# A gathered part of the expert sum grows from 512 to 768 columns and moves to SBUF, with the first norm's rows made in the query stage

## What is computed

```python
h = _layer_norm(DEEPNORM_ALPHA * h + mix, ln1_g[l], ln1_b[l])
ffn = _peer(h, w_peer_q[l], peer_subkeys[l], peer_u[l], peer_v[l])
h = _layer_norm(DEEPNORM_ALPHA * h + ffn, ln2_g[l], ln2_b[l])

# _peer: 8 heads x 16 picks a token, of 128 x 128 experts
q = (xt @ w_q).reshape(t, PEER_HEADS, 2, PEER_QDIM // 2)
scores = jnp.einsum('thpd,hpkd->thpk', q, subkeys)
...                       # top 16 of each half, top 16 of their sums
act = jax.nn.gelu(jnp.einsum('tkd,td->tk', u_tab[eb], xb))
out = jnp.einsum('tk,tkd->td', gb * act, v_tab[eb])
```

## Time and profile before

| | us |
|---|---|
| median of 3 runs (lowest, highest) | 1992.04 (1989.96, 1997.78) |
| the profiled execution | 1982.38 |
| its span, first to last instruction | 1980.5 |
| PE busy | 1945.3 (98%) |
| DVE busy | 1314.3 (66%) |
| POOL busy | 1427.6 (72%) |
| ACT busy | 989.6 (50%) |

### The profile page before, as it was taken

How to read it: one execution, slowest core, us unless ns; L and a number is a source line. 1 busy time by engine, 2 the same in 40 slices (tenths; PEclk the granted TensorE clock), 3 DMA queues, 4 the chain that set the end, 5 groups by cost and what they waited for, 6 DMA issues and landing times.

```text
span 1980.5 us, 34370 instructions
## 1 busy us (share of the span) xinstructions
PE 1945.3 (98%) x10830; PEld 1692.5 (85%) x10830; DVE 1314.3 (66%) x2299; ACT 989.6 (50%) x1518; POOL 1427.6 (72%) x978
## 2 busy tenths in 40 slices
PE   9999999999999999999999999999999998999996
PEld 8999888889998888888888888888888886787885
DVE  1744102212778887756899999986777776787776
ACT  5544334435455566575455554555555554454553
POOL 6877778887779989898788778765266665677601
PEclk9999999999999999999999999999999999999999
DMA  9555657577869888688877777768788888778872
GB/s 301 172 149 169 193 160 225 180 204 189 190 141 212 190 184 193 157 196 203 221 175 175 175 168 175 173 165 291 253 295 283 294 290 324 272 264 309 288 248 116
DMA packets 178186, 423.82 MB, mean 214 GB/s; under 512 B 27248, under 2 KB 38384, under 8 KB 159808
## 3 DMA queue, kind: packets, MB, share of 16 engines
q1 hardware_dynamic: 162688, 384.52, 68.5%
q0 software_dynamic: 14416, 33.83, 4.9%
q10 hardware_dynamic: 1008, 4.52, 0.7%
HBM read 410.01 MB, written 12.78 MB: 213 GB/s over the span
## 4 chain that ended last, share of the span: by engine, by line
PE 79%; POOL 9%; issue 6%; DMA 2%; DVE 1%; SPq 1%; ACT 1%; DVEq 0%; POOLq 0%; ACTq 0%
PE ps L1761 29%; PE ps L1720 16%; PE ps L1721 8%; PE ps L1460 7%; PE ps L1462 7%; PE ps L1461 7%; POOL u_lo L1377 6%; PE ps L1702 3%; POOL w_lo L1339 2%; DMA v_raw<-in_peer_v 1%; DMA u_raw<-in_peer_u 1%; PE ps L1576 1%; SPq L355 0%; DMA raw<-in_w_in 0%; PE ps L1685 0%
## 5 line engine op out<-in xcount | busy, mean ns | idle before, releaser
L1377 POOL TENSOR_TENSOR u_lo<-u_t,u_hi 128x512 fp32r<-128x512 f32 x512 | 653.1, 1299 | 128.5 <-ACT u_hi L623 126.3
L1720 PE MATMUL ps<-xT,u_hi 128*128 128x512 f32 x2048 | 724.1, 398 | 0.9 <-POOL u_lo L1377 0.9
L1721 PE MATMUL ps<-xT,u_lo 128*128 128x256 f32 x2048 | 571.4, 279 | 0.0
L1339 POOL TENSOR_TENSOR w_lo<-raw,w_hi 128x1024 fp32r<-128x1024 f32 x174 | 424.0, 2447 | 106.0 <-ACT w_hi L492 99.6
L623 ACT ACTIVATE u_hi<-u_t 128x512 fp32r<-128x512 f32 x512 | 321.0, 632 | 350.4 <-DVE u_t L1021 350.0
L1720 PEld LDWEIGHTS ps<-xT,u_hi 128*128 128x128 f32 x2048 | 384.4, 188 | 89.5 <-issue 1.2
L1021 DVE STREAM_TRANSPOSE u_t<-u_raw 128x512 f32<-128x512 f32 x512 | 355.0, 701 | 99.0 <-PE ps L1721 59.1
L1721 PEld LDWEIGHTS ps<-xT,u_lo 128*128 128x128 f32 x2048 | 386.0, 188 | 0.0
L492 ACT ACTIVATE w_hi<-raw 128x1024 fp32r<-128x1024 f32 x175 | 184.8, 1059 | 272.1 <-PE ps L1462 265.2
L1761 PE MATMUL ps<-v_hi,m_hi 128*128 128x512 f32 x896 | 291.2, 393 | 14.5 <-DVE m_lo L1250 10.3
L1761 PE MATMUL ps<-v_hi,m_lo 128*128 128x512 f32 x896 | 289.6, 391 | 0.0
(11 more groups left out here) (224 smaller groups left out, 2629.1 us busy)
## 6 DMA issues: line engine op xcount, KB each, us to landing
u_raw<-in_peer_u SPq DMA_DIRECT2D x512, 256.0 KB, 4.9
v_raw<-in_peer_v SPq DMA_DIRECT2D x126, 1024.0 KB
raw<-in_w_in SPq DMA_DIRECT2D x111, 512.0 KB, 3.8
raw<-in_w_out SPq DMA_DIRECT2D x32, 512.0 KB, 4.4
raw<-in_w_peer_q SPq DMA_DIRECT2D x128, 128.0 KB, 3.7
act_dram<-act_w ACTq DMA_DIRECT2D x4, 1024.0 KB, 6.4
act_dram<-far_act SPq DMA_DIRECT2D x64, 64.0 KB, 5.1
x_again<-in_x SPq DMA_DIRECT2D x1, 2048.0 KB, 8.0
```

The lines of the kernel that those rows point to most:

```text
L1339: pool.tensor_tensor(w_lo[:, k, :], raw[:, k, :], w_hi[:, k % HI_RING, :].bitcast(F32), ALU.subtract).then_inc(lo_done, 1)
L1377: pool.tensor_tensor(u_lo[:, r, :], u_t[:, r, :], u_hi[:, r, :].bitcast(F32), ALU.subtract).then_inc(ulo_done, 1)
L1720: pe.matmul(acc, u_hi[:, r, c], xT[:, :, kt, :], start=kt == 0, stop=False)
L1721: ins = pe.matmul(acc[:, 0:T], u_lo[:, r, c], xT_hi[:, kt, :], start=False, stop=kt == KT - 1)
```

## The change

The gathered part becomes 768 columns wide (`FAR`), so that it covers all of bank 7 and half of bank 6, and is summed in SBUF (`far_sum`). The products for token half 1, side 1 are made on 256 columns instead of 512. The first picks are added beside tile 8 instead of tile 16. The rows for the second norm are no longer made by POOL in the V stage: DVE makes them in the query stage (four operations of 2048 columns), SP stores these rows (`h1_dram`) instead of `n_perm`, and they come back in four pieces, each behind one tile's transfer. `ln2b_sb` comes in two pieces in the same way, directly after, `ln2g_sb` in two pieces once the gathered sum is done. The gain and shift of the first norm are loaded ahead of the query weights. The transfers of tiles 126 and 127 stand behind those of 122 and 123, one each. POOL makes the second power ahead of its parts for bank 3.

```diff
-S_CHUNK, S_FIRST = 5, 4
+FAR = 768
+S_CHUNK, S_FIRST = 5, 2
...
             sp.dma_start(sk_raw[:], subkeys[0].rearrange("h s k d -> k (h s) d")).then_inc(sk_in, 16)
+            sp.dma_start(ln1g_sb[:], ln1_g[0:1, :].to_broadcast([P, D])).then_inc(ln1_rows_in, 16)
+            sp.dma_start(ln1b_sb[:], ln1_b[0:1, :].to_broadcast([P, D])).then_inc(ln1_rows_in, 16)
...
                 if g == O_END + 1:
-                    sp.wait_ge(n_block, 10)
-                    sp.dma_start(n_dram.rearrange("(a p) d -> p a d", p=P), n_perm[:]).then_inc(n_out, 16)
+                    sp.wait_ge(h1_made, TT)
+                    sp.dma_start(h1_dram.rearrange("(a p) d -> p a d", p=P), h1_rows[:]).then_inc(h1_out, 16)
...
-            sp.dma_start(n_again[:], n_dram.rearrange("(a p) d -> p a d", p=P)).then_inc(n_in, 16)
-            sp.dma_start(ln1g_sb[:], ln1_g[0:1, :].to_broadcast([P, D])).then_inc(n_in, 16)
-            sp.dma_start(ln1b_sb[:], ln1_b[0:1, :].to_broadcast([P, D])).then_inc(n_in, 16)
-            with sp.Fori(P // 8 + 1, P // 4 - 7) as ii:
+            for ii in range(P // 8 + 1, P // 8 + 3):
                 for s in range(4):
                     sp.wait_ge(v_free, ii * 8 + 2 * s + 2)
                     load_v(ii * 4 + s, s)
+                    beside((ii - P // 8 - 1) * 4 + s)
...
-            sp.wait_ge(row_added, P)
-            for s in range(2):
-                sp.dma_start(v_late_raw[...], v_rows[P - 2 + s]...).then_inc(v_late, 16)
+            sp.wait_ge(far_added, 1)
+            for h in range(2):
+                sp.dma_start(ln2g_sb[:, half_row(h)], ln2_g[0:1, half_row(h)].to_broadcast([P, HALF])).then_inc(last_in, 16)
+            for s in range(4):
+                sp.wait_ge(v_free, (P // 4 - 2) * 8 + 2 * s + 2)
+                load_v(P - 8 + s, s)
+                if s >= 2:
+                    sp.dma_start(v_late_raw[...], v_rows[P - 4 + s]...).then_inc(v_late, 16)
...
+            dve.wait_ge(ln1_rows_in, 32)
+            for a in range(TT):
+                dve.tensor_tensor(part(h1_rows[:, a, :], 0, KT), in_perm(n_perm[:, a, :], 0, KT), part(ln1g_sb[:], 0, KT), ALU.mult)
+            dve.drain()
+            for a in range(TT):
+                dve.tensor_tensor(h1_rows[:, a, :], h1_rows[:, a, :], ln1b_sb[:], ALU.add).then_inc(h1_made, 1)
...
-                dve.scalar_tensor_tensor(bank(7), sp_rows[:, c, :], sp_w[...], bank(7), ALU.mult, ALU.add).then_inc(row_added, 1)
+                dve.scalar_tensor_tensor(far_sum[:], sp_rows[:, c, :], sp_w[...], far_sum[:], ALU.mult, ALU.add).then_inc(row_added, 1)
...
+            far = h1_again[:, 1, D - FAR:]
+            dve.scalar_tensor_tensor(far, far, float(ALPHA), far_sum[:], ALU.mult, ALU.add).then_inc(far_added, 1)
...
-                if n > 13 and n < 22:
-                    h1_block((n - 14) // 4, (n - 14) % 4)
...
             ln_power(3, slice(0, 1))
             last_rest(0, 2, 1)
+            ln_power(4, slice(1, 2))
             last_rest(0, 3, 2)
-            ln_power(4, slice(1, 2))
             last_rest(1, 3, 3)
...
-                        ins = pe.matmul(bank(4 * a + 2 * h + c), m, v[:, c * 512:(c + 1) * 512], ...)
+                        n = COL if (a, h) != (1, 1) else HALF - FAR
+                        ins = pe.matmul(bank(4 * a + 2 * h + c)[:, 0:n], m, v[:, c * COL:c * COL + n], ...)
```

74 lines of the change are left out of this document (35 added, 39 removed).

## The result

The changed kernel took 1960.5 us (median of 4 runs, 1959.4 to 1966.5) against 1991.5 us of the kernel before beside it (4 runs, 1990.0 to 1997.8): a ratio of 0.9845 with a 95% interval of 0.9815 to 0.9874, 31 us faster. Timed a second time it was 1958.5 against 1986.9, 0.9859 (0.9835 to 0.9882). The forecast was 1946 with a range of 1926 to 1968, and a gain of 45.6 us. So sign and range held, and the gain was a third smaller than forecast.

The account below looks back on a forecast made before the run. TensorE at its full rate was taken to bound the V stage. The terms, -39.7 - 16.9 - 1.7 - 2.3 + 3 + 4 + 8 = -45.6 us, took 1992.0 to 1946 us, range 1926 to 1968.

Parts of the forecast that it names:

- What bounds the kernel: V stage: nearly all of it is TensorE at full rate, 4.76 us a tile of 21 products.
- the three stalls: V stage, tile 68 and two places with `h1_block`: TensorE's missing products come back with the causes removed, -16.9 us.
- Narrower products: V stage: 3 of 21 products at 256 columns make a tile 4.44 us, -39.7 us over the first 124 tiles.
- rival of no gain: V stage: narrow products don't get cheaper between wide ones, +39.7, 1986 us; chance 0.05.
- Query stage: DVE's four row operations put POOL back and TensorE stalls: +3 us, ends 0 and +8 (2 MB ahead of query weights).
- The pieces: Tiles 68 to 73: 0.52 MB more a tile puts the DMA queue back, a stall and the clock behind it, +4 us.
- The wider rows: Row phase: longer DVE adds and slower POOL gathers leave little room, 0.3 us a chunk over 26 chunks, +8 us.
- The end of +34: Row phase: upper end of the cost of 768-column rows, where a chunk stays at 19.04 us.
- Last tiles: Tile 125's transfer: two late tiles asked for earlier, the queue empties before it, -2.3 us, ends 0 and -4.4.
- Last norm: Kernel's end: POOL's second power ahead of its bank 3 parts lets DVE go on earlier, -1.7 us.
- locked gathers: Row phase: each gather starts as a DVE operation begins and takes 2.28 us, 2069 us in all; chance 0.07.
- The slow chunk: Row phase: DVE and POOL set the pace, 18.5 us a chunk, +24 instead of +8, 1962 us; chance 0.17.

Follow-up runs that it names:

- Experiment 7: Changed kernel with FAR = 512, so that all 21 products of a tile are 512 columns wide and rows too; 1972.7 us, ratio 0.9931.
- experiment 2: Changed kernel with gain and shift of the first norm loaded behind the first group of query weights; 1959.2 us, ratio 0.9876.
- experiments 5 and 6: Changed kernel with 512-column gathers but 768-column adds: 1948.8 us, 0.9806; and with 768-column gathers but 512-column adds: 1951.0 us, 0.9826.
- experiment 8: Changed kernel with side 0 of all four last tiles made first, side 1 of tiles 125 to 127 after them; 1956.0 us.

## Why the prediction was right, and where it was not

- **What bounds the kernel**: right. TensorE's rate sets a tile, and the three stalls are gone with their causes (17.3 us in the table, -16.9 forecast). Experiment 7 shows it at the old pace, with 0.9 us left. The two causes near tile 100, `h1_block` and the 1 MB of `ln2b_sb`, were removed together and are not told apart.
- **Narrower products**: 4.46 us instead of 4.44, -37.2 instead of -39.7 over 124 tiles. The rival of no gain falls.
- **Query stage**: +3, measured +6.4 and +5.6 (4.0 and 3.2 at the copy of tile 8, where the tiles ahead have already saved 2.4). The step that failed is the choice of mechanism. The two queued megabytes ahead of the weights, which I kept as the end of +8, are the main cause: without them 2.2 are left (experiment 2). The turns of GpSimd and VectorE at the port, which I took for the value, are there but reach TensorE with 0.74 us; the other 1.5 have no cause shown.
- **The start of the rows**: +7 us, and no term in my sum. "The first picks are added beside tile 8" stood in my list of edits with no price. A start that is moved forward must be held against the time at which its producer is ready: the list, ten gathers of 1.5 us with the gap, 5.5 us for the row itself. The trace of the kernel before had it: first row asked for at 1368.1, with tile 8's copy of `m_hi` at 1370.3.
- **The pieces**: +4, measured +4.3 and +5.0. Right in size; nothing with FAR = 512, and with the pieces spread between 0.0 and 5.9, so that they are a part of the load and not the cause alone.
- **The wider rows**: +8, measured 10.0 and 11.6 (columns 10-66 and 76-114). The size was near, the mechanism wrong. I looked for a GpSimd that is full; its gathers stayed at 1.2 us and rows were never late between 1440 and 1640. What is late is `v_raw`. My sum even had both numbers: 7.2 us from the free slot to ScalarE's wish, and 7 us for a transfer. I spent them on the pieces, and did not hold the steady wider gathers against the same margin. Nor did I put the late tile and VectorE's full loop together: it takes both (experiments 5 and 6). The end of +34 should have been 33 by its own terms.
- **Last tiles**: -2.3, measured +2.3 and -0.8 (the table's +1.7 and -1.4, with the 0.6 taken out that two faster tiles save). The step that failed was that tile 124 alone gives the queue time to empty before 125. The queues were still full when that transfer was issued, and with one of the two late tiles asked for some 4 us earlier ahead of it, it took no less:

```profile
1908.18 7.38 DMA v_raw<-in_peer_v
```

The stretches around it, DMA share and GB/s last:

```profile
1906.00:1908.00 2.00, 2.00 (x12) 1.69 (x12) 0.90 (x2) 1.06 (x1) 0.00 (x0) 1.00 1.01 369
1908.00:1912.00 4.00, 4.00 (x20) 3.31 (x19) 2.41 (x3) 2.18 (x3) 0.00 (x0) 1.00 0.92 338
1912.00:1916.00 4.00, 4.00 (x21) 3.35 (x20) 2.69 (x3) 1.92 (x4) 0.00 (x0) 1.00 0.16 61
```

  Some 1.6 MB moved until it landed, of which 1.05 are its own. And what bounded there besides was VectorE's order of the low parts, with the clock behind it (experiment 8): 14 products at 0.43 us instead of 0.23 are some 2.8 us, which the kernel before did not pay.
- **Last norm**: -1.7, measured +2.1. The new order is worth 1.5 us, as I thought, but a wait of 2.27 us ahead of it became 4.75, and VectorE's wait for the power, which was to be gone, is 3.17 us after 3.05.
- **Sum**: of the 23 us between -45.6 and -22.6, 6.8 stand at the first rows, 4.6 in the last tiles, 3.8 in the last norm, 3.4 in the query stage, 2.5 in the narrow products and 2.0 in the wider rows. All of these had one sign. The timed median came out nearer (15 us off, not 23), and that is luck: the profiled execution before lay 9.7 us under its median, the one after 0.9, a difference that I had carried over as if it belonged to the kernel.
- **Rivals**: locked gathers (2.28 us each) don't occur. The slow chunk (18.5 us, 1962) gave nearly the right time by a wrong cause.

On the two rules that I had weighed. The changed kernel moved 409 GB/s over the 20 us from 1660, so the 358 GB/s of the Trainium skill ("DMA: Bandwidth & Descriptors", section "Where 436 GB/s comes from") is no limit that this trace keeps to. Yet the steady row phase, at 337 to 344 GB/s, already pays for late tiles. As a warning near 350 the figure would have served better than my reading of it as refuted. The port rule (the Trainium skill, "SBUF — State Buffer", section "Who interferes with whom") speaks against a sum in SBUF; experiment 7 has that sum in SBUF with 0.9 us of stalls, so with rows of 512 columns it cost nothing that reaches TensorE.

## What to carry to other kernels

When the bounding engine gets faster, recompute each lead time in tiles, not only each engine's load: a transfer that takes 7 us and is asked for 1.6 tiles ahead had margin at 4.76 us a tile, and came late at 4.46 with wider gathers beside it. A late input hurts only where the next engine has no room to catch up, so look at both. If a buffer comes free in parts, ask for it in parts; that was worth 14 to 18 us here, about as much as the step to wide rows itself. And whatever is moved to an earlier place needs its own check of when its inputs are ready.
